# Two pieces of matrix work moved across the borders of the attention stage in a fused decoder step on one core

## What is computed

```python
h = rms(x) * (1 + scale) + shift
(u_h, u_b, u_c, z_a, q, k, v, qi, ki, wi, z_b, g_a, g_b) = split(h @ w_in)
# per block of 128 queries: the indexer keeps the 256 best keys of each query
logits = einsum(q, k_sel) * HEAD_DIM ** -0.5            # 8 heads, 2 key heads
p = softmax(where(valid, logits, NEG_INF))
branch_b = einsum(p, v_sel) * silu(z_b)
merged = sigmoid(g_a) * (branch_a @ w_pa) + sigmoid(g_b) * (branch_b @ w_pb)
y = x + gate * (merged @ w_out)
```

## Time and profile before

| | |
|---|---|
| median of 3 runs | 3170.58 us (3168.75 to 3171.72) |
| the profiled execution's own time | 3169.02 us |
| its span (first to last instruction) | 3166.5 us |
| mean granted PE clock in it | 0.998 |
| busy share of the span: PE, PEld, DVE, ACT, POOL | 98%, 85%, 60%, 38%, 28% |

### The profile page before, as it was taken

One profiled execution on the slowest core, in us unless ns is written; L12 is line 12 of the kernel. 1 busy time (PEld: TensorE's weight loads), 2 busy tenths in 40 slices (PEclk: granted clock), 3 DMA queues, 4 the chain that ended last, 5 costly groups with the idle time before them and its releaser, 6 DMA issues.

```text
span 3166.5 us, 47679 instructions
## 1 busy us (share of the span) xinstructions
PE 3104.5 (98%) x18495; PEld 2700.8 (85%) x18495; DVE 1914.2 (60%) x3864; ACT 1213.6 (38%) x2116; POOL 900.4 (28%) x829
## 2 busy tenths in 40 slices
PE   6999999999999999999999999999999999999999
PEld 6999999967998888888888888889888788889987
DVE  5443697044434995048256999268527788868862
ACT  3445332345324221145334221155426444226551
POOL 2345775454520332023200331111310133111110
PEclk9999999999999999999999999999999999999999
DMA  8765688775974555631754556620563455660016
GB/s 299 260 214 196 210 277 290 263 267 170 306 249 160 195 197 199 236 125 50 281 174 143 211 190 212 229 70 13 215 225 114 166 193 195 213 232 14 11 74 235
DMA packets 266529, 599.31 MB, mean 189 GB/s; under 512 B 17693, under 2 KB 177623, under 8 KB 216130
## 3 DMA queue, kind: packets, MB, share of 16 engines
q1 hardware_dynamic: 255796, 558.38, 51.2%
q0 software_dynamic: 10368, 37.75, 3.5%
q10 hardware_dynamic: 142, 0.13, 0.0%
HBM read 453.65 MB, written 142.57 MB: 188 GB/s over the span
## 4 chain that ended last, share of the span: by engine, by line
PE 90%; DVE 4%; POOL 2%; ACT 2%; issue 2%; DMA 1%; ACTq 0%; SPq 0%; DVEq 0%; POOLq 0%
PE ps L1254 83%; PE ps L1259 6%; DVE PTL L2307 1%; POOL BBL L2708 1%; POOL WLH L2516 0%; DVE SC L2084 0%; DMA WR<-in_w_proj_b 0%; DVE LP L2324 0%; DMA WR<-in_w_in 0%; ACT PTH L1121 0%; DMA ST<-in_state_conv 0%; DVE OB L2335 0%; DVE RS L2040 0%; DMA GB<-gb_scratch 0%; POOL KT L2690 0%
## 5 line engine op out<-in xcount | busy, mean ns | idle before, releaser
L1254 PE MATMUL ps<-HTH,WLH 128*128 128x512 f32 x3504 | 1129.7, 391 | 0.0
L1254 PEld LDWEIGHTS ps<-HTH,WLH 128*128 128x128 f32 x3504 | 657.8, 188 | 139.7 <-issue 5.8
L1254 PE MATMUL ps<-HTL,WLH 128*128 128x512 f32 x1752 | 682.2, 389 | 0.0
L2159 DVE TENSOR_SCALAR_CACHE_REDUCE JUNK<-SC,SMALL 128x1920 bf16<-128x1920 f32 (+5 forms) x364 | 514.2, 1413 | 17.0 <-POOL SC L2594 3.9
L1254 PE MATMUL ps<-H,WLH 128*128 128x288 f32 x3504 | 483.2, 298 | 6.1 <-POOL WLH L2516 2.1
L1254 PEld LDWEIGHTS ps<-H,WLH 128*128 128x128 f32 x3504 | 473.1, 190 | 8.5 <-POOL WLH L2516 2.9
L1254 PEld LDWEIGHTS ps<-HTL,WLH 128*128 128x128 f32 x1752 | 329.1, 188 | 66.0 <-issue 0.7
L2324 DVE CUSTOM_DVE_ANT_0 LP<-ps,SC,RQ 128x512 f32<-128x512 f32 (+3 forms) x320 | 202.4, 666 | 298.9 <-PE ps L1254 298.4
L963 ACT ACTIVATE T<-ps 128x512 f32<-128x512 f32 x192 | 114.7, 597 | 649.3 <-PE ps L1254 637.8
L2516 POOL TENSOR_TENSOR WLH<-WR,WLH 128x1024 fp32r<-128x1024 f32 x97 | 234.4, 2416 | 312.8 <-ACT WLH L779 312.7
L2084 DVE SCALAR_TENSOR_TENSOR SC<-T,WI,SC 128x512 f32<-128x512 f32 (+3 forms) x266 | 179.2, 698 | 119.8 <-ACT T L897 119.2
(11 more groups left out here) (370 smaller groups left out, 5172.6 us busy)
## 6 DMA issues: line engine op xcount, KB each, us to landing
WLH<-w_scratch SPq DMA_DIRECT2D x291, 1024.0 KB, 4.9
w_scratch<-WLH SPq DMA_DIRECT2D x97, 1024.0 KB, 5.5
WR<-in_w_in SPq DMA_DIRECT2D x73, 512.0 KB, 4.4
MW<-in_w_mod SPq DMA_DIRECT2D x6, 2048.0 KB, 16.1
q_scratch<-QO SPq DMA_DIRECT2D x32, 256.0 KB, 5.7
ma_scratch<-T SPq DMA_DIRECT2D x32, 256.0 KB, 5.6
gb_scratch<-GB SPq DMA_DIRECT2D x32, 256.0 KB, 5.9
QU<-q_scratch SPq DMA_DIRECT2D x64, 128.0 KB, 2.2
```

Source lines behind the costliest of these rows:

```text
L1254: return pe.matmul(out, lhsT, rhs, start=start, stop=stop, **more)
L2159: ins_ = dve.tensor_scalar(JUNK[0:n, 0:row.shape[1]], row, MID[0:n, c:c + 1], 0.0, ALU.is_ge, ALU.add, accum_out=CNT[0:n, c:c + 1])
```

## The change

Tile 0 keeps its order. In tiles 1 to 3:

- PE: the logits of unit 0 come ahead of the last `zb` item, and steps 0 to 3 of the first `pb` item come between `lengths` of unit 14 and the values of unit 15.
- To allow this, the probabilities of unit 0 and of units 14 and 15 get memory of their own (LP_FIRST, LP_LAST), DG and TB move, `attn_low` of k = 1 and 3 moves from DVE to POOL, and the bank of each item is chosen anew, so that the last `zb` item has bank 3.
- ACT: `exponentials` of unit 0 ahead of the copy out of the last `zb` item; `attn_high` in pairs: k = 0, 1 after the exponentials of unit 14, k = 2, 3 ahead of those of unit 15, k = 4, 5 ahead of unit 15's last copy.
- POOL: `whole_keys` in two halves, one per key head: the first after `diagonals` of unit 13, the second last of all. `attn_low` of 0 and 1 after `diagonals` of unit 14, of 2 and 3 ahead of `diagonals` of unit 15.
- DVE: in unit 15 `finish` of unit 14 comes ahead of the low part of group 3.

```diff
+    LP_FIRST = at("LP_FIRST", [P, 2, SEQ], F32, rM)
+    LP_LAST = [at(f"LP_LAST{i}", [P, 2, SEQ - TILE], F32, rS + 12288 * i) for i in range(2)]
+    LP_LAST3 = [at("LP_LAST30", [P, 2, SEQ], F32, rS), at("LP_LAST31", [P, 2, SEQ], F32, rKH)]
...
+    EARLY = range(4)
+    on_dve = lambda t, k, p: p == "P" and k % 2 == 1 and not (t and k in EARLY)
...
@@ ACT attend
+            last = len(UNITS) - 1
+            for u in range(len(UNITS)):
+                if u == last:
+                    attn_high(t, (2, 3))
+                if u:
                     exponentials(t, u)
+                if u == last - 1:
+                    attn_high(t, (0, 1))
+                if u and u + 2 < len(UNITS):
                     query_high(t, u + 2)
+                for c in range(unit_groups(t, u)):
+                    if u == last and c == unit_groups(t, u) - 1:
+                        attn_high(t, (4, 5))
+                    copy_p(t, u, c)
+                if u == 0:
+                    query_high(t, 2)
...
@@ ACT, gating items
-                if i == len(PROJ_B) - 1:
+                if i == len(PROJ_B) - 2:
                     query_high(t, 0)
                     query_high(t, 1)
+                if t and i == len(PROJ_B) - 1:
+                    exponentials(t, 0)
...
@@ PE
+                if t and i == len(PROJ_B) - 1:
+                    head_logits(t, 0)
                 products(j)
...
-                head_logits(t, 0)
                 for u in range(len(UNITS)):
                     if u + 1 < len(UNITS):
                         head_logits(t, u + 1)
                     if u:
                         lengths(t, u - 1)
+                    if u == len(UNITS) - 1:
+                        products(j, steps=EARLY)
                     head_values(t, u)
             for f in range(KC):
...
+                elif f == 0:
+                    products(j, steps=range(len(EARLY), KC))
...
@@ DVE attend
-                for c in range(1, groups if groups <= 4 else 3):
+                early = 3 if groups > 4 or u == len(UNITS) - 1 else groups
+                for c in range(1, early):
                     probabilities_low(t, u, c)
...
-            attn_low(t, 1)
             finish(t, len(UNITS) - 1)
...
-                for k in (3, 5, 7):
+                for k in (5, 7):
                     attn_low(t, k)
...
@@ POOL
-                    if u == len(UNITS) - 2 and t + 1 < TILES:
-                        whole_keys(t)
-                for k in (0, 2, 4, 6):
+                    if u == last:
+                        attn_low(t, 2)
+                        attn_low(t, 3)
+                    diagonals(t, u)
+                    if u == last - 2 and t + 1 < TILES:
+                        whole_keys(t, 0)
+                    if u == last - 1:
+                        attn_low(t, 0)
+                        attn_low(t, 1)
+                for k in (4, 6):
                     attn_low(t, k)
+                if t + 1 < TILES:
+                    whole_keys(t, 1)
```

More of the change, by code:

```diff
@@ L84, in parts, with product_bank @@
     return ("P", "S") if t == 0 else ("P",)
-PRODUCTS = [(j, p) for j, (t, n, f) in enumerate(GEMMS) for p in parts(t)]
-PBANK = {jp: i % 4 for i, jp in enumerate(PRODUCTS)}
+FIRST_BANK = {1: 2}
+def product_bank(j):
+    t, i = divmod(j, WEIGHTS)
+    before_out = len(PROJ_A) + len(PROJ_B)
+    if t == 0:
+        return 2 * (i % 2)
+    if i == before_out - 1:
+        return 3
+    return (i - before_out if i >= before_out else i + FIRST_BANK.get(t, 0)) % 4
+PBANK = {(j, "P"): product_bank(j) for j in range(len(GEMMS))}
 class Signal:
@@ L319, in program @@
     R4 = [r[:, :].bitcast(F32) for r in R4R]
-    DG = at("DG", [P, 4, P], F32R, rKH + 6144)
-    TB = [at(f"TB{i}", [P, 256], F32, rKL + 6144 + 1024 * i) for i in range(2)]
+    DG = at("DG", [P, 4, P], F32R, rGT)
+    TB = [PFX[:, 0:256], PFX[:, 256:512]]
     PT = [[at(f"PT{i}", [P, TILE], F32, rM + 8192 + 2048 * i) for i in range(3)]] + [T[0:3]] * (TILES - 1)
@@ L1106, in exponentials @@
                 act.wait_ge(*row_max.at(t, u, hh))
-                row = LP[t][:, u % 2, hh, 0:w]
+                row = probabilities(t, u)[:, hh, 0:w]
                 act.activation(row, row, ACT.Exp, bias=NM[:, u % 2, hh:hh + 1],
@@ L1123, in attend @@
         def attend(t):
-            for u in range(len(UNITS) + 1):
-                if u < len(UNITS):
+            last = len(UNITS) - 1
[3 more added lines that the diff above has]
+                if u:
                     exponentials(t, u)
-                if u + 2 < len(UNITS):
+                if u == last - 1:
+                    attn_high(t, (0, 1))
+                if u and u + 2 < len(UNITS):
                     query_high(t, u + 2)
[L1129 to L1133, removed]
+                for c in range(unit_groups(t, u)):
+                    if u == last and c == unit_groups(t, u) - 1:
+                        attn_high(t, (4, 5))
+                    copy_p(t, u, c)
+                if u == 0:
+                    query_high(t, 2)
         def attn_high(t, ks):
@@ L1138, in attn_high @@
                 act.wait_ge(*attn_z.at(t, (BLOCKS - 1, k // 2)))
-                if k == 0:
-                    act.wait_ge(*(pv.at(t, len(UNITS) - 2) if t else s_pv.at(PAIRS[-1], 3)))
+                if t == 0 and k == 0:
+                    act.wait_ge(*s_pv.at(PAIRS[-1], 3))
                 act.activation(part(t, "BB", 0, k, "P"), paired(t, BBT[t][:, k, :]), ACT.Copy).then_inc(*bb_high.mark(t, k, "P"))
@@ L2378, in attend @@
                     finish(t, u - 1)
-                if groups > 4:
-                    probabilities_low(t, u, 3)
-                for c in range(4, groups):
+                for c in range(early, groups):
                     probabilities_low(t, u, c)
-            attn_low(t, 1)
             finish(t, len(UNITS) - 1)
         def attn_low(t, k):
-            if t and k == 1:
-                dve.wait_ge(*p_t.at(t, len(UNITS) - 1, unit_groups(t, len(UNITS) - 1) - 1))
             dve.wait_ge(*bb_high.at(t, k, "P"))
@@ L2683, in key_low, with whole_keys @@
                                ).then_inc(*k_split.mark(t, f))
-        def whole_keys(t):
-            pool.wait_ge(*qk.at(t, len(UNITS) - 1))
-            for f in range(KC):
-                kv, cols = key_quarter(t, f)
+        def whole_keys(t, kv):
+            pool.wait_ge(*qk.at(t, len(UNITS) - (1 if kv else 3)))
+            for f in range(kv * KC // KV, (kv + 1) * KC // KV):
+                cols = key_quarter(t, f)[1]
                 ins_ = pool.tensor_tensor(KT[:, kv, cols], KLOW[:, kv, cols].bitcast(F32), KHIGH[:, kv, cols].bitcast(F32), ALU.add)
-            ins_.then_inc(*k_whole.mark(t))
+            if kv == KV - 1:
+                ins_.then_inc(*k_whole.mark(t))
         def query_low(t, u):
@@ L2763, in _ @@
             else:
+                last = len(UNITS) - 1
                 for u in range(len(UNITS)):
-                    if u + 2 < len(UNITS):
+                    if u and u + 2 < len(UNITS):
                         query_low(t, u + 2)
+                    if u == last:
+                        attn_low(t, 2)
+                        attn_low(t, 3)
                     diagonals(t, u)
-                    if u == len(UNITS) - 2 and t + 1 < TILES:
-                        whole_keys(t)
-            if t:
-                for k in (0, 2, 4, 6):
+                    if u == 0:
+                        query_low(t, 2)
+                    if u == last - 2 and t + 1 < TILES:
[4 more added lines that the diff above has]
+                for k in (4, 6):
                     attn_low(t, k)
+                if t + 1 < TILES:
+                    whole_keys(t, 1)
             for f in range(KC):
```

30 lines of the change are left out of this document (19 added, 11 removed).

## The result

| | before | changed |
|---|---|---|
| median of 5 runs each, side by side | 3170.47 us (3168.75 to 3171.72) | 3183.33 us (3182.5 to 3187.36) |
| the profiled execution's span | 3166.5 us | 3180.5 us |
| mean granted PE clock | 0.998 | 0.996 |

What follows compares the result with a forecast made beforehand. PE was busy 98% of the span, so only its standing still could be won. Tiles 1 to 3 summed +2.9, +1.45, -1.15, together +3.2 us: 3172.2 profiled, 3173.8 as median; range 3167.0 to 3178.5.

Steps and rivals of the forecast that it cites:

- Start of the stage: Start of attention in tiles 1 to 3: last zb item covers unit 0's logits, exponentials and table load; gain 1.2 us together.
- The tables: Rival: ACT's engine drains at each table load, so PE waits; +2.6 us added, 3176.4 us in all; chance 0.05.
- Half item in tile 1: Ahead of unit 15 in tile 1: POOL's four BBL lead PE, so unit 15's turns start 5.5 us later.
- Nothing won: Inside unit 15 of tile 1: the last PTL pair starts 7.0 us behind the turns, as before.
- Half item in tiles 2 and 3: Ends of tiles 2 and 3: unit 15 starts 1.75 and 1.15 us later; second pb item gains 2.1 us in each.
- From x to the second item: From x, the last PTL pair's start, to the second pb item: 5.25 us; gains 1.8, 2.1 and 2.1 in tiles 1 to 3.
- Late keys: KT's second half behind BBL 6 delays SP's weight loads; PE waits 3.0 us in tile 2, nothing in tile 1.
- KT late hurts in both tiles: Rival: late weights cost 1.8 us more in tile 1, 1.5 more in tile 2; +6.5 us in sum; chance 0.20.
- that bound of 4.5: Upper bound in us on PE's late-weight wait in tile 2, if the three loads add their own time.
- Its own signs: Waits expected if right: BBL in tile 1's half item and steps 5 to 7, exponentials in tile 3, WLH in tile 2.

Runs made afterwards that it cites:

- copy-first kernel: Changed kernel with unit 2's query (SP, POOL), BBL 0 and 1, and keys moved earlier, and tile 1's BBH 4, 5 behind unit 15's last copy: 3166.89 us, ratio 0.9984.

## Why the prediction was wrong

It was wrong by 8.7 us in the sum (3.2 against 11.9), and 5.4 of these lie in one term.

- *Start of the stage: the step that failed.* The term said: "The query load that ACT sat on for 1.08 us is behind the copies now. Gain 1.2 in the three tiles together; ends of this term 0.5 and 1.6". Measured: +3.5, +0.6 and about +0.1, a loss of 4.2 instead of a gain of 1.2. I moved PE's logits ahead of an item and took it that their supply moved too. Neither SP's load nor POOL's `query_low` of unit 2 did: the one stayed behind a wait for the item that PE now does later, the other was put behind `diagonals` of unit 0. The second move stood in the full diff and is missing from the account of it. The ends of the term shut out a loss though two queues had not been followed. The sign is sure, the size is not: the same order gave +2.4 to +4.9 in tile 1, by the clock. With both put right five kernels give -0.6 in tile 1, against -0.8 less 0.1 to 0.2 for the table load in the forecast: the sum's own mechanism was right.
- *The tables.* A wait of 0.21 us behind the last load: the rival falls. The load takes 1.28 us and the next exponential starts 0.01 behind it. The Trainium skill, "ScalarE: Activation LUTs", What ACT_TABLE_LOAD costs, has 1.28 us for the load, which the trace agrees with, and 1.38 more for draining, 2.66 in all; the draining is not borne out here.
- *Half item in tile 1.* Forecast +5.5 at unit 15's turns; 5.9 measured (7.3 behind DG instead of 1.4). POOL led as said, with 1.25 us per BBL instead of 1.29, so the last operand came 0.2 earlier than computed; PE then took 0.5 us more over the last steps, at the lower clock, which stood in no term (the two kernels at full clock put it at 0.4). "Nothing won" inside unit 15 was right: the wait for BBH 4 and 5 is there, 1.59.
- *Half item in tiles 2 and 3.* Forecast -1.35 and -1.15, measured -1.4 and -0.6 (0.3 of the difference lie in the middle of tile 3's stage). Right, and in tile 2 by its terms too: the turns start 1.8 us later behind `lengths` (1.75 forecast), x comes 1.05 sooner behind them (1.0), the second item 2.2 sooner behind x (2.1).
- *From x to the second item.* 5.25 us forecast; 5.45 in tile 1. DVE's BBL 5 was done 2.1 behind x instead of 2.3 (0.68 us, not 1.0), POOL's BBL 6 at 3.5 (3.65 computed), DVE's BBL 7 at 4.1 (4.2 computed).
- *Late keys: the second step that failed.* "PE waits 3.0 us in tile 2, nothing in tile 1": these stretches are 3.4 and 2.1 longer. The rival "KT late hurts in both tiles" had 1.8 for tile 1 and was right on it; I had given it 0.20. What was wrong is the time of item 5's weights in tile 1: I took 13.1 us from the issue of item 4's to the landing of item 5's, from rows in which item 4's weights were not late; it was 15.6 (1512.37 to 1528.01), near tile 2's 15.3. Of the kernels with late keys here tile 2 lost between 2.9 and 7.3 us, so even that bound of 4.5 was low; their waits for WLH were 2.6 to 3.45, and most of the rest is the clock, which fell behind five of the seven. The five runs with the keys first, leaving out the one with x four items later, show that it is the keys: in tile 1 0.2 or less is left, in tile 2 0.3 to 0.6 in four of them.
- *Its own signs.* The forecast's signs for "right" nearly all came: waits for POOL's BBL in tile 1's half item, 0.73 us for the exponentials at tile 3's end, waits for BBL in steps 4 to 7, a wait for WLH in tile 2 (2.92 us) 16.6 us behind the second item. Unit 15 of tile 1 started 4.9 us behind the half item's first matmul (1492.50), and not within 3. None of them looked at the start of the stage, so they could not tell that the sum was wrong.

What stays open: why a wait is followed by the lower clock in one execution and not in another, and how much of the 5.7 us between the medians of the copy-first kernel and of before is the 2.2 that the stretches show. The rest lies ahead of tile 1 or in other executions.

## What to carry to other kernels

When work is moved ahead on one engine, list every queue that feeds it, and for each ask what its instruction stands behind; a supply that could come earlier comes earlier only if its place in its own program moves too. Two late suppliers of one operand hide each other: undoing the later one wins only its lead over the other (0.65 us here), undoing the earlier one nothing, undoing both 4.1; the idle time of the engine between them says which is which. And half an item that fills a wait paid here (2.5 us) only once the engine that makes its operands used its own idle time for them; before that, taking it out left tile 1's end 2.7 us shorter.

## What the runs showed that was not expected

- *Waits cost twice.* A wait of PE of some 1.6 to 3.5 us can be followed by several us at 1.2 GHz, so that about as much again is lost; matmuls of 512 columns then start 0.43 us apart instead of 0.23. The length of the wait does not settle it: behind 1.79 and 1.80 us at tile 1's start the clock fell, behind 3.44 us at tile 3's end, in the kernel without the half item, it did not. Behind a wait of 2.92 us for WLH in tile 2 the changed kernel kept its clock; behind 3.05 us at the same place the kernel with both query orders lost it (windows of the two, from 2276 or 2282 us on):

```profile
2282.00:2288.00 6.00, 4.71 (x21) 3.88 (x22) 1.81 (x3) 0.60 (x1) 2.57 (x2) 1.00 1.04 416
```
```profile
2276.00:2282.00 6.00, 2.95 (x9) 2.05 (x8) 2.12 (x4) 0.60 (x1) 1.26 (x1) 0.73 1.03 413
2282.00:2288.00 6.00, 6.00 (x21) 4.75 (x20) 2.62 (x5) 0.00 (x0) 2.53 (x2) 0.70 0.75 296
```

- *DVE beside POOL.* The writers of BBL in the changed kernel, answering to the earlier trace rows:

```profile
L2746 POOL TENSOR_TENSOR BBL<-BB,BBH x18: 1262/1286/1301, 1491.1 to 3087.4; 128x512 fp32r<-128x512 f32 x18
L2429 DVE TENSOR_TENSOR BBL<-BB,BBH x6: 681/1016/1354, 1505.6 to 3087.8; 128x512 fp32r<-128x512 f32 x6
```

DVE's takes 0.68 us alone and up to 1.35 beside POOL, while none of POOL's 18 is slowed. In each tile DVE's second one starts behind POOL's (1506.94 against 1506.46 in tile 1) and ends 0.55 us behind its end, little less than the 0.68 that it takes alone: DVE hardly gets on until POOL is done. Where three of DVE's ran against POOL's, before, both were slowed. I had taken 997 ns for undisturbed; it was not.
